# Routing in three parts with column-wise one-hots, and a last combination spread over four engines

## The reference

```python
def route(t, router_w, router_bias):                    # t: tokens x 1024
    scores = sigmoid(t @ router_w)                      # 32 experts = 8 groups x 4
    grouped = (scores + router_bias).reshape(T, 8, 4)
    best = argmax(top_k(grouped, 2)[0].sum(-1))         # one group for each token
    _, local = top_k(grouped[arange(T), best], 2)       # the best two in it
    experts = best[:, None] * 4 + local
    gates = take_along_axis(scores, experts)
    return experts, gates / gates.sum(-1, keepdims=True)

# grouped_moe: the 2560 pairs (token, expert) are sorted by expert, each expert's share is
# padded to blocks of 128 rows (dest = a pair's row), every block goes through its expert,
# and a token's two rows are summed with its gates
out = segment_sum(y * row_w[:, None], row_tok)

x = layer_norm(ALPHA * x + (1.0 + gate) * out, ln_g, ln_b)   # after each sub-layer
```

## Time and profile before

| | |
|---|---|
| median of 3 runs | 3654.83 us (3649.93 to 3659.3) |
| the profiled execution | 3652.89 us, span 3651.1 us |
| PE busy | 3152.7 us, 86% of the span |
| DVE busy | 2013.3 us, 55% |
| ACT busy | 1217.5 us, 33% |
| POOL busy | 513.1 us, 14% |

### The profile page before, as it was taken

One profiled execution on the slowest core, in us unless ns is written; L12 is line 12 of the kernel. 1 busy time (PEld: TensorE's weight loads), 2 busy tenths in 40 slices (PEclk: granted clock), 3 DMA queues, 4 the chain that ended last, 5 costly groups with the idle time before them and its releaser, 6 DMA issues. The chain is left out here.

```text
span 3651.1 us, 41024 instructions
## 1 busy us (share of the span) xinstructions
PE 3152.7 (86%) x14464; PEld 1977.4 (54%) x14464; DVE 2013.3 (55%) x4016; ACT 1217.5 (33%) x2938; POOL 513.1 (14%) x517
## 2 busy tenths in 40 slices
PE   8999999689999996997795999969977889599980
PEld 3555555378888885996353444434433445344430
DVE  3886685399999973885675000045445534400008
ACT  1112221244445442663662222222245523122112
POOL 0000100100000001211000110011067800010011
PEclk9999999689999986998896999989989999699995
DMA  7453233501111102242532999943234342499975
GB/s 262 157 187 114 65 114 117 191 30 34 38 38 38 36 16 77 86 147 88 176 134 91 348 404 382 362 145 134 75 107 115 115 131 100 141 399 368 359 282 193
DMA packets 360749, 583.79 MB, mean 160 GB/s; under 512 B 50358, under 2 KB 255702, under 8 KB 360314
## 3 DMA queue, kind: packets, MB, share of 16 engines
q1 hardware_dynamic: 287480, 346.93, 28.7%
q0 software_dynamic: 34560, 123.47, 9.4%
q10 hardware_dynamic: 38532, 111.10, 7.8%
HBM read 456.75 MB, written 124.68 MB: 159 GB/s over the span
## 5 line engine op out<-in xcount | busy, mean ns | idle before, releaser
L364 PE MATMUL inp__bank<-inp__hT,inp__w 128*128 128x512 f32 (+1 forms) x1536 | 559.5, 523 | 1.0 <-DVE inp__hT L508 1.0
L2655 PE MATMUL moe__bank<-kept__weights,moe__xT 128*128 128x512 f32 x1024 | 457.4, 600 | 12.5 <-DMA kept__weights<-in_moe_w_up_dram 8.3
L364 PEld LDWEIGHTS inp__bank<-inp__hT,inp__w 128*128 128x128 f32 x1536 | 289.2, 190 | 254.3 <-issue 240.0
L2655 PEld LDWEIGHTS moe__bank<-kept__weights,moe__xT 128*128 128x128 f32 x1024 | 191.0, 192 | 237.0 <-issue 234.9
L2115 PE MATMUL close__bank<-kept__weights,kept__catT 128*128 128x512 f32 x640 | 286.3, 602 | 16.4 <-ACT kept__catT L2220 7.7
L2773 DVE TENSOR_TENSOR moe__hid<-moe__sg,moe__bank 128x256 f32<-128x256 f32 x64 | 26.9, 421 | 478.5 <-ACT moe__sg L2716 478.5
L2672 PE MATMUL moe__bank<-moe__wdn,moe__hidT 128*128 128x512 f32 x512 | 230.5, 593 | 2.9 <-ACT moe__hidT L2720 2.9
L3023 PE MATMUL cq__bank<-kept__w_in,cq__hT 128*128 128x512 f32 x480 | 211.9, 598 | 2.9 <-DVE cq__hT L3159 2.9
L3402 POOL TENSOR_SCALAR attn__p<-attn__p,attn__rec 128x384 f32<-128x384 f32 x160 | 195.7, 1244 | 117.9 <-DVE attn__rec L3377 117.9
L2115 PEld LDWEIGHTS close__bank<-kept__weights,kept__catT 128*128 128x128 f32 x640 | 121.1, 193 | 163.4 <-issue 143.9
L433 ACT ACTIVATE inp__z<-inp__bank 128x512 f32<-128x512 f32 (+1 forms) x96 | 50.4, 525 | 404.9 <-PE inp__bank L364 404.9
(11 more groups left out here) (469 smaller groups left out, 5846.6 us busy)
## 6 DMA issues: line engine op xcount, KB each, us to landing
kept__weights<-in_moe_w_gate_dram SPq DMA_DIRECT2D x64, 1024.0 KB, 8.1
kept__weights<-in_moe_w_up_dram SPq DMA_DIRECT2D x64, 1024.0 KB, 14.8
moe__wdn<-in_moe_w_down_dram ACTq DMA_DIRECT2D x64, 1024.0 KB, 8.2
inp__wv<-in_ada_w_dram SPq DMA_DIRECT2D x10, 4096.0 KB, 15.9
scratch_y_rows<-moe__y ACTq DMA_DIRECT2D x64, 512.0 KB, 8.6
scratch_zt<-inp__tb SPq DMA_DIRECT2D x32, 640.0 KB, 4.9
inp__w<-in_ab_w_in_dram POOLq DMA_DIRECT2D x31, 512.0 KB, 4.8
rwkv__rk<-scratch_zt SPq DMA_DIRECT2D x20, 512.0 KB, 3.8
```

What stands on the lines that cost most here:

```text
L364: mm = pe.matmul(zbank[j][g][:, 0:n], w[:, j, k, :], hT[:, k, t0:t0 + n], start=k == 0, stop=k == KC - 1)
L2655: mm = pe.matmul(bank[2 + j][:], xT[:, j, k, :], wgu[:, j, k].rearrange("p a n -> p (a n)"), start=k == 0, stop=k == KC - 1)
```

## The change

In `close_mixer`, `route` is cut in three stages (sigmoid and best group; first expert; second expert and counts) and in three parts of six, three and one tiles. All stages of the first part stand in DVE's loop, the first stage at the end of step 8 and the others at the end of step 9; the other two parts stand behind the loop. ACT's exponentials come in three pieces, at `s == 7`, at `s == NT` and at the end. `residual` handles its two halves one after the other. The block number comes from scaling and rounding instead of the comparison with all limits, and the one-hots are made pair by pair, each counted, so that PE waits for one pair at a time. In `combine`, PE forms the gated sum of the two rows as products with diagonal matrices that ACT builds from an identity, DVE multiplies the result by the gate row and adds the old row with an instruction that also sums, ACT takes the squares, and POOL makes the last addition and gathers three tiles ahead.

```diff
-    EARLY = NT - 1
+    PARTS = ((0, 6), (6, 9), (9, NT))
+    MAGIC = 1.5 * 2 ** 23
...
-                pe.wait_ge(hot_r, 1)
                 for n in range(2 * NT):
+                    pe.wait_ge(hot_r, 2 * n + 2)
                     mm = pe.matmul(bank[1][:, 0:BLOCKS], at_pos[:, n, :], in_blk[:, n, :], start=n == 0, stop=n == 2 * NT - 1)
...
+                def exp_logits(part):
+                    lo, hi = PARTS[part]
+                    act.wait_ge(lg, hi)
+                    act.activation(sc[:, 0, lo * E:hi * E], bank[6][:, lo * E:hi * E], ACT.Exp, scale=-1.0).then_inc(sg, 1)
...
+                        if s == 7:
+                            exp_logits(0)
                         shifted(s - 1)
...
+                        if c == 0:
+                            dve.wait_ge(x_l[r], 16 * (i // 3) + 16)
+                        dve.wait_ge(taken, 2 * i + c + 1)
+                        dve.scalar_tensor_tensor(x2[:, cols], x[:, r, cols], ALPHA, x2[:, cols], ALU.mult, ALU.add).then_inc(x2_r, 1)
+                        dve.wait_ge(x2_r, 2 * i + c + 1)
+                        clink(dve.bn_stats(stats[:, c], x2[:, cols]))
...
-                dve.wait_ge(router_l, 48)
-                link(dve.memset(upto[:, 0], 0.0))
-                route(0, 0, EARLY)
-                route(1, EARLY, NT)
+                    if s == 8:
+                        dve.wait_ge(router_l, 48)
+                        link(dve.memset(upto[:, 0], 0.0))
+                        route(0, 0)
+                    if s == 9:
+                        route(0, 1)
+                        route(0, 2)
+                for part in (1, 2):
+                    for stage in range(3):
+                        route(part, stage)
...
+                more(dve.tensor_scalar(lane[:, 0], places, 1.0 / P, -127.0 / 256.0, ALU.mult, ALU.add))
+                more(dve.tensor_scalar(lane[:, 0], lane[:, 0], MAGIC, None, ALU.add))
+                more(dve.tensor_scalar(lane[:, 0], lane[:, 0], -MAGIC, None, ALU.add))
...
+                for n in range(2 * NT):
+                    dve.tensor_scalar(in_blk[:, n], rank[:, 0:BLOCKS], lane[:, 0, n:n + 1], tok[:, n % NT:n % NT + 1],
+                                      ALU.is_equal, ALU.mult).then_inc(hot_r, 1)
+                    dve.tensor_scalar(at_pos[:, n], cf[:, CONST["lane"]], lane[:, 1, n:n + 1], None, ALU.is_equal).then_inc(hot_r, 1)
...
+                def gather(i):
                     if i > 2:
-                        pool.wait_ge(t_r, i - 2)
+                        pool.wait_ge(y_mm, 2 * (i - 2))
...
+                    pool.tensor_tensor(out[:, i % 3], u[:, i % 2], ln[:, 1], ALU.add).then_inc(out_r, 1)
...
+                for i in range(3):
+                    gather(i)
+                for i in range(NT):
+                    if i + 3 < NT:
+                        gather(i + 3)
+                    shifted(i)
...
+                    pe.wait_ge(dg_r, 2 * i + 2)
+                    pe.wait_ge(y_l[i % 3], 32 * (i // 3) + 32)
+                    if i > 3:
+                        pe.wait_ge(taken, 2 * (i - 3))
+                    for c in range(2):
+                        for n in range(2):
+                            mm = pe.matmul(bank[2 * (i % 4) + c][:], dg[:, i % 2, n], y[:, i % 3, n, c * 512:(c + 1) * 512], start=n == 0, stop=n == 1)
+                        mm.then_inc(y_mm, 1)
...
+                        act.activation(dg[:, i % 2, n], ident[:], ACT.Copy, scale=gates[:, n, i:i + 1]).then_inc(dg_r, 1)
...
+                    act.activation(junk[:], t[:, r], ACT.Square, bias=mv[:, r, 0:1], accum_out=mv[:, r, 1:2]).then_inc(sq_r, 1)
...
+                        dve.tensor_tensor(t[:, r, cols], bank[2 * (i % 4) + c][:], grow[:, int(i >= TP), cols], ALU.mult).then_inc(taken, 1)
+                    dve.wait_ge(taken, 2 * i + 2)
                     dve.wait_ge(x_more[r] if i > 2 else x_l[r], 16 * (i // 3) if i > 2 else 16)
-                    dve.scalar_tensor_tensor(t[:, r], x[:, r], ALPHA, t[:, r], ALU.mult, ALU.add).then_inc(t_r, 1)
+                    dve.tensor_tensor_reduce(t[:, r], t[:, r], x[:, r], 1.0, 0.0, ALU.add, ALU.add, mv[:, r, 0:1]).then_inc(t_r, 1)
                     dve.wait_ge(t_r, i + 1)
...
+                    dve.tensor_scalar(mv[:, r, 0:1], mv[:, r, 0:1], -1.0 / D, None, ALU.mult).then_inc(mean_r, 1)
...
-                    dve.tensor_tensor(out[:, r], out[:, r], ln[:, 1], ALU.add).then_inc(out_r, 1)
+                    if i > 1:
+                        dve.wait_ge(out_r, i - 1)
+                    dve.tensor_tensor(u[:, i % 2], t[:, r], ln[:, 0], ALU.mult).then_inc(u_r, 1)
```

More of the change, by code:

```diff
@@ L2257, in _ @@
                     if s == NT:
-                        act.wait_ge(lg, EARLY)
-                        act.activation(sc[:, 0, 0:EARLY * E], bank[6][:, 0:EARLY * E], ACT.Exp, scale=-1.0).then_inc(sg, 1)
+                        exp_logits(1)
                     if have(s + 2):
@@ L2270, in _ @@
                             act.wait_ge(cols_r, 1)
+                        if s == 7:
+                            exp_logits(0)
                         shifted(s - 1)
-                act.wait_ge(lg, NT)
-                act.activation(sc[:, 0, EARLY * E:W], bank[6][:, EARLY * E:W], ACT.Exp, scale=-1.0).then_inc(sg, 1)
+                exp_logits(2)
             @block.vector
@@ L2376, in columns, with route @@
                     link(dve.tensor_scalar(grow[:], grow[:], 1.0, None, ALU.add))
-                def route(part, lo, hi):
-                    dve.wait_ge(sg, part + 1)
+                def route(part, stage):
+                    lo, hi = PARTS[part]
                     nt = hi - lo
@@ L2388, in route @@
                     m0, m1, m2, m3 = (r1[:, n, lo:hi] for n in range(4))
[L2389 to L2402, removed]
@@ L2415, in route @@
+                    if stage > 0:
+                        c = stage - 1
                         chosen, weight = r4[:, 2 + c, wp], r4[:, 5, wp]
@@ L2429, in route @@
                                                by_tile(chosen, PER).unsqueeze(2).broadcast_to([P, nt, GROUPS, PER]), ALU.mult))
-                    link(dve.tensor_tensor(place[:, lo:hi], one[:, 0, lo:hi], one[:, 1, lo:hi], ALU.add))
-                    for t in range(lo, hi):
-                        link(dve.tensor_tensor(upto[:, t + 1], upto[:, t], place[:, t], ALU.add))
+                    if stage == 2:
+                        link(dve.tensor_tensor(place[:, lo:hi], one[:, 0, lo:hi], one[:, 1, lo:hi], ALU.add))
+                        for t in range(lo, hi):
+                            link(dve.tensor_tensor(upto[:, t + 1], upto[:, t], place[:, t], ALU.add))
                 means(0)
@@ L2508, in _ @@
                 dve.wait_ge(idx_mm, 1)
-                more(dve.tensor_scalar(past[:, 0, 0:BLOCKS], bank[1][:, 0:BLOCKS], 0.25, None, ALU.add))
-                more(dve.tensor_copy(idx[:], past[:, 0, 0:BLOCKS]))
+                more(dve.tensor_scalar(in_blk[:, 0], bank[1][:, 0:BLOCKS], 0.25, None, ALU.add))
+                more(dve.tensor_copy(idx[:], in_blk[:, 0]))
             @block.gpsimd
@@ L2837, in _ @@
             def _(pool):
-                for i in range(NT):
+                def gather(i):
                     if i > 2:
-                        pool.wait_ge(t_r, i - 2)
+                        pool.wait_ge(y_mm, 2 * (i - 2))
                     for c in range(2):
@@ L2857, in norm_rows @@
                     act.activation(t[:, r], t[:, r], ACT.Identity, scale=mv[:, r, 2:3], bias=mv[:, r, 3:4]).then_inc(n_r, 1)
-                weigh(0)
+                diagonals(0)
+                diagonals(1)
                 for i in range(NT):
-                    if i + 1 < NT:
-                        weigh(i + 1)
+                    squares(i)
                     norm_rows(i)
+                    if i + 2 < NT:
+                        diagonals(i + 2)
             @block.vector
@@ L2911, in _ @@
                         finished(i - 1)
+                    variance(i)
                     scaled(i)
```

121 lines of the change are left out of this document (69 added, 52 removed).

## The result

The changed kernel takes 3619.23 us (median of 4 runs, 3612.14 to 3622.97) against 3655.61 beside it: a ratio of 0.9908, 95% interval 0.9894 to 0.9923. The forecast was 3619.6. The profiled execution took 3620.23 us, its span is 3618.4 against 3651.1. The stages show that this agreement holds less than it seems.

A forecast was written before the change was run, and what follows sets the result against it. VectorE was taken to set the end of the last combination and of each close phase. Routing 19.5 plus combination 15.7 gave 35.2 us off 3652.89, so 3617.7, with 1.9 for the median 3619.6; range 3608 to 3638.

The forecast's parts named there:

- One-hots and the chain: End of each close phase: two DVE instructions fewer gain 0.4 us a layer, one-hots in pairs 5.6 a layer.
- Routing in layer 0: Layer 0's close phase: routing in parts starts the last part 5.4 us earlier, PE's delay costs 1.9, so 3.5 gained.
- Routing in layer 1: Layer 1's close phase: routing in parts lets the last part start at 3121.47 + 0.19 instead of 3125.73, 4.0 us gained.
- The cover: Layer 1's loop: DVE's wait for PE's next projection hides the moved six-tile routing, with 1.1 us to spare.
- The combination: Last stage, spread over four engines: 5.9 us a tile, 5.0 later at the start, 2.0 at the end, 15.7 gained.
- Three rates of 5.2, 5.7 and 5.8 feed each other: Combination: DVE's chain 5.2 us a tile, POOL 5.7, transfers 5.8; together taken as 5.9, bounds 5.2 and 8.3.
- four products at the start and what follows: Combination's first tile: PE's products take 7.5 us at the lower clock, 13.2 from landing to last small instruction, 5.0 later.
- A: Rival, combination: POOL's add and DVE's two-SBUF-input instructions don't run together, 8.3 us a tile; total gain 18.3, 3636.5; chance 0.14.
- B: Rival, combination: PE stays at the lower clock level, 7.5 us a tile; total gain 20.7, 3634.1; chance 0.08.
- C: Rival, one-hots: a pair takes the upper bound, 0.61 us, 3.8 a layer less; total gain 27.6, 3627.2; chance 0.13.
- D: Rival, combination: transfers and POOL don't limit, 5.2 us a tile; total gain 41.5, 3613.3; chance 0.17.
- E: Rival, combination: the add on POOL is dear; at 8.3 us each the kernel is 11 us slower, 3666; chance 0.04.

## Why the prediction was right, and where not

**The total** lay in the range and near the middle, but 25 of the forecast's 35.2 us are found in the stages. Two terms were too large, the routing's and the combination's, and what filled the gap lies outside the edited stages: in part differences between executions, the rest open. The hit of 0.4 us is luck.

**One-hots and the chain** (forecast 6.0 a layer): from the last part's first instruction to the index read 34.73 us before and 28.47 after in layer 1, 34.74 and 28.46 in layer 0: 6.3. The pair takes 0.41 (0.42 worked out), the index read stands 11.63 behind (11.7), and DVE sets it, as said. The row to price the 128-wide compare by was the right one.

**Routing in layer 0** (3.5): the last part starts 242.5 us into the phase and started at 244.9, a gain of 2.4. The delay of PE was forecast at 1.9. PE idles for 2.12, but its projection starts only 1.4 later in the phase than before (205.9 against 204.5). What the sum missed is that the product behind the idle time then takes 8.80 in place of 7.13: 1.7 more. The granted clock says why: 0.81 on the mean of this product, where the kernel before has 1.00 (1926.20 to 1933.33) and so has the run that takes the half first. That run gave both back, 4.3. The loss need not fall on this product: in five later profiles with the same wait it takes 7.10 or 7.11 at 1.00, as in the run with the one-input product,

```profile
1928.93 7.10 PE L2116 MATMUL close__bank<-kept__weights,kept__catT 128*128 128x512 f32 x16 [2.13 <-DVE close__x L2348]
1949.39 3.62 PE L2132 MATMUL close__bank<-close__rw,close__hT 128*128 128x32 f32 x16 [3.00 <-ACT close__hT L2239]
```

and the ninth tile's router product (the second row, at a granted clock of 0.50) takes 3.62, where it takes 2.03 in the changed kernel. The phase lasts 272.5 to 272.8 in all eight.

**Routing in layer 1** (4.0): the last part starts 195.4 into the phase against 196.5, 1.1 gained. The cover held by 1.1 us, as forecast: the half residual ended 158.0 into the phase, and PE's projection began at 159.05. The rest was lost at the phase's start. DVE's first instruction on PE's result came 21.3 us into the phase and not 20.2, behind a load of norm weights, and the product block after it took 15.67 in place of 13.97. Windows of the block, after and before:

```profile
2937.18:2952.85 15.67, 15.67 (x34) 6.86 (x35) 8.55 (x14) 2.73 (x3) 0.61 (x1) 0.89 0.22 78
2950.21:2964.18 13.97, 13.97 (x34) 6.27 (x35) 6.80 (x11) 2.73 (x3) 0.61 (x1) 1.00 0.30 109
```

The longer block has the lower granted clock, 0.89, behind 2.25 us of PE's idle time and not 1.18. That block took 13.97 in all three profiles with the old close phase. In ten with the new one it took 13.97 four times, 15.67 five times and 16.99 once. PE idled 1.9 to 4.2 us ahead of it in these ten and 1.2 to 2.7 in the three, and the length does not follow the idle time. Whether the change makes the long block likelier isn't settled.

**The combination** (15.7, measured 9.3): the tile was mis-sized, 5.9 forecast and 6.6 measured, by the reciprocals' mean distance. "Three rates of 5.2, 5.7 and 5.8 feed each other": DVE's chain was 6.24, since 1.5 of wait was missing in it; POOL's list and ACT's diagonals coupled tiles on top. From the first small product's end to the last one's, which is what the sum counts, it took 61.15 us and not 53.1, so 8.0 of the forecast's gain is missing; another 1.1 is lost because the first rows landed 7.7 us into the phase and not 6.5. Two terms were too careful: four products at the start and what follows took 11.65 us from the landing to the first small product's end (13.2 forecast), the end cost 0.7 (2.0).

**The rivals.** A named the right thing and the wrong victim: POOL and DVE do get in each other's way, but the addition keeps its 2.34 us, while DVE's smallest two-input instruction waits for it. Its 8.3 a tile did not come. The Trainium skill (GPSIMD Engine Reference, "Specifications") says that the two share SBUF interfaces, with contention for DVE's instructions with two SBUF inputs; the trace agrees, by 1.66 against 0.16 and 0.21. B: in part. PE's eight records took 3.67 in three of the last six tiles and 5.4 to 6.2 in the others, at a granted clock of 0.59 to 0.68. "A PE that is late works without a pause" failed: PE was late because it waited for ACT's diagonals, the clock was lower behind that wait, and DVE then waited 0.5 to 1.4 us for PE's second half. So the clock has a part in the long tiles; how much wasn't tried. C: no, a pair took 0.41. D: 5.2 wasn't reached; with three edits more it was 5.43. E: the addition takes 2.34. For it I took 3.2. The 2.25 estimated from the Trainium skill (GPSIMD Engine Reference, "Performance versus the Vector engine") was nearer; the trace agrees with it to 0.1.

## What to carry to other kernels

Where GpSimd gets wide arithmetic, list all of VectorE's instructions that may meet it in time, small ones above all, and give those on the path a form with one tensor input, or an input in PSUM. Look the other way too: here gathers issued by GpSimd were held by VectorE's wide two-input instructions. An engine's list is an order: a gather behind an addition waits for all that the addition waits for, so look at who is queued behind each new wait. And compare a change by the stages that it edits, with the same kernel profiled twice beside it: a total can agree for the wrong reasons.

## What the runs showed of the hardware

- A product of two 128x1 tensors on VectorE took 1.64 to 1.67 us in the changed kernel under a POOL addition of two 128x1024 tensors and ended with it; with a per-partition scalar in place of the second tensor it took 0.21, and multiplications of PSUM by SBUF (0.64 a half) were not held. A 128x1024 sum of two SBUF tensors took 2.07 where the addition had 0.98 us to go, and 1.22 alone.
- The other way, POOL's gathers take up to 1.97 us in place of 0.94. All 62 that began under a wide VectorE instruction with two inputs from SBUF ended 0.81 to 0.83 us after it, and the other 198 took at most 0.96; no run changed this alone.
- After 2.12 us of idle time TensorE took 8.80 us for a projection of 7.13, at a granted clock of 0.81 in place of 1.00. That was so in three of eight profiles with this wait; in the other five the projection took 7.10 or 7.11 at 1.00, and the clock fell at a later product.
- The recurrence, the same code in all kernels, took from 714.8 to 729.1 us in thirteen profiles.
